# A two-layer block on one core: the first layer's last out projection placed among the third block's projections, and attention scores ordered behind the transposes of two units back

## What is computed

```python
# first layer
h = x @ w_in                                  # 1024 -> 3584
y = concat([sgu(...), conv(...), hgrn2(...)]) # each times silu(gate)
x = layernorm(ALPHA * x + y @ w_out)          # the out projection
# second layer
p = rmsnorm(x) @ w_in_2                       # 1024 -> 2560: pool input, q, k, v of both attentions
a = pool_mixer(...)
b = diff_attention(...)    # 4 heads: (softmax(q1 k1') - lam * softmax(q2 k2')) v, causal
c = stick_breaking(...)    # 4 heads, in pairs: sigmoid(z) times a reversed running product of 1 - sigmoid(z)
x = x + concat([a, b, c]) @ w_out_2
x = x + (silu(h2 @ w_gate) * (h2 @ w_up)) @ w_down ; out = rmsnorm(x)
```

## Time and profile before

| | |
|---|---|
| median of 3 runs | 3848.14 us (3844.67 to 3849.72) |
| profiled execution | 3846.98 us, its span 3844.6 us |
| mean granted TensorE clock | 0.988 of full speed |
| TensorE busy | 3722.9 us, 97% |
| VectorE, ScalarE, GpSimd busy | 1826.5, 1418.3, 476.1 us |

### The profile page before, as it was taken

The page is one execution under the profiler, slowest core; times in us unless marked ns, Lnnn a source line. Parts: engine busy times, 40 slices in busy tenths (PEclk is TensorE's granted clock), DMA queues, the critical chain, the costliest instruction groups (busy, mean ns, idle before and its releaser), DMA issues.

```text
span 3844.6 us, 58659 instructions
## 1 busy us (share of the span) xinstructions
PE 3722.9 (97%) x24136; PEld 3101.4 (81%) x24136; DVE 1826.5 (48%) x3358; ACT 1418.3 (37%) x2534; POOL 476.1 (12%) x244
## 2 busy tenths in 40 slices
PE   8989999999999989899999999999999999999999
PEld 7878878978897878787778887788888777887887
DVE  5757625551644353445665544555454454232223
ACT  4322422231232343465555545444455443021001
POOL 2102130000000000233433301000001000000000
PEclk9999999999999999899999999999999999999999
DMA  8746677557655858677677664455555333564554
GB/s 309 264 164 225 240 258 264 200 212 243 222 193 193 280 202 269 208 242 248 224 237 247 207 215 165 159 167 169 171 189 181 122 144 132 205 225 175 197 189 162
DMA packets 198874, 799.34 MB, mean 208 GB/s; under 512 B 20816, under 2 KB 70224, under 8 KB 130384
## 3 DMA queue, kind: packets, MB, share of 16 engines
q1 hardware_dynamic: 198608, 795.59, 59.4%
HBM read 594.18 MB, written 201.33 MB: 207 GB/s over the span
## 4 chain that ended last, share of the span: by engine, by line
PE 89%; DVE 4%; ACT 2%; DMA 2%; issue 1%; POOL 0%; SPq 0%; DVEq 0%; ACTq 0%
PE bank L1393 85%; PE bank L1397 4%; DVE P L2472 1%; DVE R L2133 0%; SPq L2676 0%; ACT L1927 0%; DMA Y2d<-PY 0%; ACT P L1928 0%; POOL slot L2636 0%; ACT P L1927 0%; DVE P L2474 0%; DMA zraw<-in_x_t_dram 0%; DMA R<-in_x_n_dram 0%; DMA slot<-Wd 0%; DVE small L2462 0%
## 5 line engine op out<-in xcount | busy, mean ns | idle before, releaser
L1393 PE MATMUL bank<-Z1a,slot 128*128 128x512 f32 x3048 | 785.0, 402 | 10.7 <-DVE slot L2071 9.5
L1393 PE MATMUL bank<-Z1b,slot 128*128 128x512 f32 x3048 | 786.8, 402 | 3.2 <-DVE Z1b L2180 3.2
L1393 PE MATMUL bank<-slot,Z0b 128*128 128x512 f32 (+1 forms) x3504 | 713.0, 353 | 14.8 <-DVE R L2133 12.0
L1393 PEld LDWEIGHTS bank<-Z1a,slot 128*128 128x128 f32 x3048 | 565.8, 190 | 141.3 <-DVE slot L2071 9.5
L1393 PEld LDWEIGHTS bank<-Z1b,slot 128*128 128x128 f32 x3048 | 567.4, 190 | 138.7 <-issue 8.7
L1393 PEld LDWEIGHTS bank<-slot,Z0b 128*128 128x128 f32 x3504 | 559.9, 188 | 110.5 <-DVE R L2133 16.6
L2636 POOL TENSOR_TENSOR slot<-raw,slot 128x1024 fp32r<-128x1024 f32 x117 | 295.9, 2536 | 714.3 <-ACT slot L1811 714.3
L2133 DVE SCALAR_TENSOR_TENSOR R<-bank,small,R 128x512 f32<-128x512 f32 x352 | 260.3, 748 | 207.5 <-PE bank L1393 207.0
L1393 PE MATMUL bank<-KS,DQ 128*128 128x512 f32 (+3 forms) x960 | 279.7, 390 | 23.5 <-ACT P L1928 11.8
L2440 DVE TENSOR_SCALAR_CACHE_REDUCE P<-bank 128x512 f32<-128x512 f32 (+3 forms) x320 | 187.7, 607 | 224.2 <-PE bank L1393 222.7
L2648 POOL TENSOR_TENSOR Z0b<-AF,Z0b 128x512 fp32r<-128x512 f32 x88 | 130.5, 1483 | 1282.1 <-ACT Z0b L2001 1282.1
(11 more groups left out here) (233 smaller groups left out, 4416.1 us busy)
## 6 DMA issues: line engine op xcount, KB each, us to landing
slot<-Wd SPq DMA_DIRECT2D x390, 1024.0 KB, 5.0
Wd<-slot SPq DMA_DIRECT2D x130, 1024.0 KB, 7.4
raw<-in_wts_dram SPq DMA_DIRECT2D x130, 512.0 KB, 4.2
DQ<-Qd SPq DMA_DIRECT2D x192, 128.0 KB, 3.7
DV<-Vd SPq DMA_DIRECT2D x60, 256.0 KB, 4.8
Kd<-QS SPq DMA_DIRECT2D x24, 512.0 KB, 5.2
Qd<-QS SPq DMA_DIRECT2D x24, 512.0 KB, 7.3
KS<-Kd SPq DMA_DIRECT2D x24, 512.0 KB, 7.0
```

The lines of the kernel that those rows point to most:

```text
L1393: return e.matmul(o, a, b, start=start, stop=stop, skip_group_check=True)
```

## The change

Seven things are edited. (1) The eight tiles of B for block 3 are used between tile 13 and 14 of C2 (`C_CUT`), and `phase_b(S - 1)` is called there from `phase_c`, no longer after it. (2) `front` may place the scores of unit u when the transposes of unit u - 2 are placed (`tr`, which free the buffer P), no longer when its output is copied out (`o`). (3) `SLACK_F` falls from 1000 to 300. (4) The planned VectorE time of a stick-breaking unit falls from 300 + 4.3 n to 300 + 3.5 n ns, n being its keys. (5) Q, K and V of blocks 1 and 2 are staged in `raw` (`staged`), those of 0 and 3 stay in `QS`, with waits to match: ScalarE waits once for the last first-use weights ahead of block 1, and the load of the first two E tiles waits for the stores of block 2 (`heads_stored`). (6) The load of residual rows (`r in`) is placed when the pooling of the block before is done. (7) The loops of `phase_c` are written as one. Instructions, their sizes and their numbers stay, and line numbers shift by up to 14 (L1393 is L1402 in the changed kernel, L1397 is L1406).

```diff
--- before.py
+++ after.py
@@ -40,6 +40,7 @@
 T_A, T_B, T_C, T_E, T_F = 0, 28, 36, 56, 64
 N_TILES = 64 + N_F
 NSLOT, NRAW = 4, 2
+C_CUT = 14
 
 
 class Signal:
@@ -172,9 +173,10 @@
     for s in range(S):
         for part in first_layer(s):
             order += TILES[part]
-        if s > 0:
+        if s == S - 1:
+            order += [*range(T_C, T_C + C_CUT), *range(T_B, T_B + N_B), *range(T_C + C_CUT, T_C + N_C)]
+        elif s > 0:
             order += range(T_C, T_C + N_C)
-    order += range(T_B, T_B + N_B)
     order += range(T_C, T_C + N_C)
     for s in range(S):
         order += range(T_E, N_TILES)
@@ -197,7 +199,7 @@
             for qt in range(NT)]
 
 
-SLACK_H, SLACK_C, SLACK_F, SLACK_B = 1500.0, 2000.0, 1000.0, 2500.0
+SLACK_H, SLACK_C, SLACK_F, SLACK_B = 1500.0, 2000.0, 300.0, 2500.0
 
 
 class Order:
@@ -533,7 +535,9 @@
 
 
     def phase_b(self, s):
-        self.dma(("r in", s), 2097152, self.P.end.get(("C gone", s - 1), 0.0))
+        if s:
+            yield ("pl y", s - 1, 1)
+        self.dma(("r in", s), 2097152, self.P.end.get(("pl y", s - 1, 1), 0.0))
         last = s == self.S - 1
         zr = [("zs", "Y", s, j) for j in (0, 1, 3, 2)]
         for cg in range(4):
@@ -587,17 +591,14 @@
                 yield ("pl halo", s - 1)
             yield from self.fm(("C", s, n), T_C + n, 1, zr, ("act", 610))
         P.add(self.pooling(s), slack=SLACK_C)
-        for n in range(2, 10):
-            yield from self.fm(("C", s, n), T_C + n, 1, zr, *kq)
+        for n in [*range(2, 10), 10, 12, *range(14, 18), 18]:
+            if (s, n) == (self.S - 2, C_CUT):
+                yield from self.phase_b(self.S - 1)
+            if n in (10, 12, 18):
+                yield from self.pair([("C", s, n, p) for p in range(2)], T_C + n, 1, zr, vv)
+            else:
+                yield from self.fm(("C", s, n), T_C + n, 1, zr, *kq)
             self.stored(s, n)
-        for n in (10, 12):
-            yield from self.pair([("C", s, n, p) for p in range(2)], T_C + n, 1, zr, vv)
-            self.stored(s, n)
-        for n in range(14, 18):
-            yield from self.fm(("C", s, n), T_C + n, 1, zr, *kq)
-            self.stored(s, n)
-        yield from self.pair([("C", s, 18, p) for p in range(2)], T_C + 18, 1, zr, vv)
-        self.stored(s, 18)
         P.put(("C done", s))
         yield ("pl y", s, 1)
         P.put(("C gone", s))
@@ -654,7 +655,7 @@
                     self.get(i, w)
                 self.get(i + 1, ("k", 0))
             if u > 1:
-                yield ("o", u - 2)
+                yield ("tr", u - 2, (NT * self.units[u - 2][0] + self.units[u - 2][3]) // 4)
             n = SUB * s + 128 * (qt + 1)
             ws = chunks(n)
             for r in ((0, 1) if e < 4 else (half,)):
@@ -682,7 +683,7 @@
                 P.put(("cb", u), ("dve", 900 + 1.1 * n), after=t)
             else:
                 yield t1
-                P.put(("cb", u), ("dve", 300 + 4.3 * n), after=t1)
+                P.put(("cb", u), ("dve", 300 + 3.5 * n), after=t1)
 
     def back(self):
         P = self.P
@@ -895,7 +896,6 @@
                 if s + 1 < S:
                     P.add(self.split_x(s + 1), True)
                 yield from self.phase_c(s - 1)
-        yield from self.phase_b(S - 1)
         P.add(self.split_y(0, "Y2"), True)
         yield from self.phase_c(S - 1)
         for s in range(S):
@@ -1045,12 +1045,16 @@
         def rows_of(x, s):
             return x[SUB * s:SUB * s + SUB, :].rearrange("(c p) n -> p c n", p=128)
 
-        def parts_of(i, n):
+        def staged(s, i):
+
+            return raw[i] if 0 < s < S - 1 else QS[i]
+
+        def parts_of(s, i, n):
 
             if n % 2:
-                x = QS[i][:, :].rearrange("p (c a t) -> p c a t", c=NT, a=2)
+                x = staged(s, i)[:, :].rearrange("p (c a t) -> p c a t", c=NT, a=2)
                 return x[:, :, 0, :], x[:, :, 1, :]
-            return QS[i][:, 0:SUB], QS[i][:, SUB:2 * SUB]
+            return staged(s, i)[:, 0:SUB], staged(s, i)[:, SUB:2 * SUB]
 
         def heads_of(b):
             return b[:, :].rearrange("p (c t) -> p c t", c=NT)
@@ -1290,11 +1294,16 @@
         def y2_out(s, e):
             return (d_y2p if e < 2 else d_py)("Y2 out", s, e)
 
-        def staging_stored(e, s):
+        def heads_stored(e, s):
 
             for i in range(2):
                 e.wait_ge(*d_qs[i](*[qkv_of[m] for m in sorted(qkv.values()) if qkv_of[m] in d_qs[i].at and qkv_of[m][1] == s][-1]))
                 e.wait_ge(*d_qv[i](*[qkv_of[m] for m in sorted(qkv.values()) if qkv_of[m] in d_qv[i].at and qkv_of[m][1] == s][-1]))
+
+        def staging_stored(e, s):
+
+            if s in (0, S - 1):
+                heads_stored(e, s)
             e.wait_ge(*y2_out(s, 1))
             e.wait_ge(*pe_pl("pl mm", s, 1))
 
@@ -1767,10 +1776,13 @@
                     act.wait_ge(*d_qs[i](*qkv_of[m - 2]))
                     if is_v(qkv_of[m - 2][2]):
                         act.wait_ge(*d_qv[i](*qkv_of[m - 2]))
+                if s == 1:
+                    for j in plan.news[:T_E][-NRAW:]:
+                        act.wait_ge(*weights_ready(j))
                 if is_v(n):
-                    to, x = QS[i][:, 0:SUB], b[:, :]
+                    to, x = staged(s, i)[:, 0:SUB], b[:, :]
                 else:
-                    to = parts_of(i, n)[0].bitcast(F32R)
+                    to = parts_of(s, i, n)[0].bitcast(F32R)
                     x = heads_of(b) if n % 2 else b[:, :]
                 e.activation(to, x, ACT.Copy).then_inc(*act_g.inc("ev", label))
 
@@ -2691,6 +2703,8 @@
 
             def weights(j):
                 if plan.first(j):
+                    if plan.tiles[j] in (T_E, T_E + 1):
+                        heads_stored(sp, S - 2)
                     if (k := plan.news.index(j)) >= NRAW:
                         sp.wait_ge(*weights_ready(plan.news[k - NRAW]))
                     transfer(raw[raw_of(j)][:, :], wts[plan.tiles[j]], d_raw[raw_of(j)], "wf", j)
...
```

8 lines of the change are left out of this document (4 added, 4 removed).

## The result

| | median of the runs, us | runs | against before |
|---|---|---|---|
| before | 3846.40 | 3844.12 to 3849.72 | |
| changed kernel | 3793.97 | 3792.94 to 3797.90 | ratio 0.9865, 95% interval 0.9848 to 0.9882 |

The changed kernel is 52.4 us faster. I had predicted 3807 us in a range of 3790 to 3835. The sign and the range held, and the size was 13 us short: it is the time of the rival "more than forecast" (3794).

What follows compares the result with a forecast made beforehand. TensorE, 97% busy, was taken to bound the kernel, with only its idle and half-clock time to gain. 18.0 + 1.95 + 26.0 - 5.7 = 40.2 us off 3846.98 gave 3806.7, predicted as 3807 us, range 3790 to 3835.

Steps and rivals of the forecast that it cites:

- more than forecast: Rival for the whole kernel: small waits don't grow and the third E tile gains its 7 us; 3794 us, chance 0.11.
- The end of B3: Post norm ahead of C3's transposes: 34.6 us of moved matmuls cover 17.4 us needed, so 18.0 us of loss goes.
- The residual rows: Load of R for B3: it waits for the pooling alone, so TensorE's wait goes; 1.95 us gained.
- The first E tile: Ten more units of attention lead let C3 projections cover block 0's store and read back; 26.0 us of loss goes.
- That the two gains can be added, each to its edit: Unsaid in the sum: 18.0 us at B3's end and 26.0 us at the first E tile were simply added.
- What the denser order costs: Attention with less main work beside it: 13 us more small waits, less 7.3 us at the third E tile; net 5.7 us.
- in proportion to the density: From 1610 to 3252 us: the 39.0 us of small idle times grow by 0.33 of themselves, 13 us.
- 7.3 us off for E2: With all attention placed ahead of this third E tile, its 9.2 us loss should fall to the fourth's 1.9 us.
- the sign that went with it: PE waits between the first E tile and the last attention matmul should sum to 40 to 60 us.
- Switching costs the same: On TensorE, the changed lists have as many kinds of alternation, so no change in switching cost.
- Slower, by scores ahead of their free banks: Rival in all units: scores listed before their banks are free stop main work too; 3855 us, chance 0.06.
- Half given back, by products slowed beside GpSimd: Rival in F0: slowed products and sigmoids hold the scores' banks, 20 us more; 3827 us, chance 0.17.

Runs made afterwards that it cites:

- e6_cut_18: The changed kernel with B3 put later, ahead of the last value pair (C_CUT 18 instead of 14); 3830.94 us, ratio 0.9953 to before.
- e1_move_only: The changed kernel with the three attention edits undone, leaving B3's new place and the raw staging of block 2; 3876.59 us, ratio 1.0069 to before.
- e4_slack_1000: The changed kernel with SLACK_F back at 1000 instead of 300; 3805.13 us, ratio 0.9885 to before.
- e3_output_key: The changed kernel with the old key: scores of unit u again behind the output copy of u - 2; 3833.64 us, ratio 0.9958 to before.
- e2_attention_only: The kernel before with the three attention edits (transpose key, SLACK_F 300, 3.5 n) and B3 in its old place; 3849.26 us, ratio 1.0.
- e15_key_only: The changed kernel with SLACK_F 1000 and 4.3 n put back, so the move and the new key stay; 3826.44 us, ratio 0.994 to before.
- e17_cost43_slackb1500: The changed kernel with 4.3 n put back and SLACK_B, the attention back end's slack, at 1500 instead of 2500; 3813.5 us, ratio 0.9903 to before.

## Why the prediction was right, and where it was off

- **The end of B3, 18.0 us.** Measured: 18.0 to 0. The cover was larger than I had counted (38.4 us from 1354.2 to 1392.6, not 34.6), and so was the need (26.0 us, not 17.4). Cover cut short brings the hole back (e6_cut_18). The step is right.
- **The residual rows, 1.95 us, bounds 0 and 2.** Wrong, though small. SP now issues the load at 1296.01, right behind a value store of block 2, and that is still late: VectorE waits 6.48 us for it (13.24 before) ahead of its first addition. The stretch up to the end of B3 loses 9.2 us where it lost 7.2.
- **The first E tile, 26.0 us.** Measured: 26.0 to 0. The reason given, more units placed ahead of block 0's end, agrees with the count of matmuls between the two ends. The price had a second part that the prediction didn't tell apart: 9.6 of the 26.0 us lay ahead of block 0's last value matmul.
- **That the two gains can be added, each to its edit.** This was unsaid in the sum, and it is wrong. Each hole goes with its own edit, but alone each opens as much elsewhere. That nothing opened elsewhere with both in place was taken for granted and not worked out, and there the sum was lucky. Had I been asked for the move alone, it would have said 3827 us; it is 3877.
- **What the denser order costs, 5.7 us.** This is the term that was mis-sized, and it is the larger part of the 13 us. I had taken the small waits in proportion to the density (39.0 x 1.33) and 7.3 us off for E2. Measured, with the clock loss: from the first E tile to the end 46.8 + 11.9 = 58.7 us before, 35.8 + 14.1 = 49.9 us after, so 8.8 us less and not 5.7 more. The step "in proportion to the density" failed, and so did the sign that went with it: idle time from the first E tile to the last attention matmul was to be 40 to 60 us and is 27.6. The density went up and the waits on VectorE's additions fell from 12.6 to 2.8 us, those on the sigmoids from 11.8 to 2.8. The other kernels don't bear out density either: the one whose attention ends latest (e1_move_only, 3250.9) loses most in this stretch, 55.6 us, and one that ends at 2926.1 (e4_slack_1000) least, 20.9. What does size these waits is only in part shown. Without the key the additions cost TensorE 10.5 us again (e3_output_key) but the sigmoids only 3.3, and two kernels with the key (e2_attention_only and e6_cut_18) lose 45.9 and 47.5 us there, to other waits. Against the 14.5 us of this term stand 2.0 us up to the end of B3, where I had forecast 1.95 us of gain, and 3.2 us in C3, which I had not forecast. That leaves 9 us of gain beyond the sum in the traces; the other 4 us of the 13 are that the profiled execution of the changed kernel is the slowest of its runs.
- **"Switching costs the same".** This says nothing of ScalarE, whose instructions did not stay in number. All 34 instructions that ScalarE is spared are table loads, rows ACT_TABLE_LOAD that stand ahead of its activations, 1.28 us each: 238 of them before and 204 now, 43.7 us of ScalarE's time. Those ahead of the stick-breaking sigmoids, before and in the changed kernel:

```profile
L1927 ACT ACT_TABLE_LOAD x42 | 53.9, 1283 | 17.9 <-DVE P L2465 8.9 <-DVE P L2474 8.4
```
```profile
L1939 ACT ACT_TABLE_LOAD x31 | 39.8, 1283 | 13.1 <-DVE P L2486 11.4 <-DVE P L2477 1.3
```

The saving comes mostly with the key: 237 in e1_move_only, 230 in e3_output_key, 210 in e15_key_only. It is a rival reason for the smaller waits on the sigmoids that no run separates from the order of the scores. It doesn't decide the time by itself: e2_attention_only has 212 and gains nothing.

- **Slower, by scores ahead of their free banks.** It didn't come: 2.8 us of waits on L1940 in the whole of 1610 to 2875. The change does have a slower side, but another one, which I had not listed: its first half alone.
- **Half given back, by products slowed beside GpSimd.** The products were slowed as the rival says, and it cost TensorE little. All 64 of them took 120.0 us where they took 109.6; the rival counted with 32 us more. Waits of ACT for the product, in before from 1610 to 3252, then in the changed kernel from 1588 to 2876:

```profile
ACT P L1927 <- DVE P L2474: 8.8, 2, 4.5
```
```profile
ACT P L1939 <- DVE P L2486: 57.3, 17, 5.7
```

ScalarE waited 57.3 us for products where it had waited 8.8, and TensorE 7.5 us (the list of its waits above). The products grew by 10.4 us in all, so most of ScalarE's longer wait is not in the products' own length. On the shared SBUF interfaces (the Trainium skill, GPSIMD Engine Reference, section Specifications) the trace agrees as far as it did in the earlier trace rows: the products are slowed. That TensorE lost only 7.5 us I put down to the other work in its row; no run tested it.

What stays open: why C3 loses 19.9 us in e1_move_only. Its waits there are read from the trace (5.9 us for VectorE's pooling tiles, 3.8 us without a named cause, 2.8 us for staged queries), but no run changed one of them alone. Which part of the smaller waits behind the first E tile is owed to the table loads is open as well. Open too is why changes of one number (e6_cut_18, e15_key_only, e17_cost43_slackb1500) cost 20 us and more outside the place they aim at.

## What to carry to other kernels

On an engine that works strictly in order, a latency is hidden by the work that stands between its two ends in the row: count that work at each hole, before and after a change, and see on which side of the first end the time is lost. Work put ahead of both ends left the hole as it was (39.6 and 38.6 us); the same amount between them took it from 26.0 to 16.4 us. Don't add up the gains of two order edits from a trace of the kernel without them: here +27 and 0 us made -52 together, so time the halves before judging either, and after such a change try the neighbouring numbers again (one of them put back gave 3787 us).

## What the hardware showed that I had not expected

Some small loads landed late where much else was in flight. DMA view of e1_move_only from 1560 to 1595 us:

```profile
DMA packets 3702, 9.48 MB, mean 271 GB/s; under 512 B 370, under 2 KB 1906, under 8 KB 3314
...
DV<-Vd SPq DMA_DIRECT2D x2, 256.0 KB, 14.9
```

Value rows of 256 KB took 14.9 us to land there. In the kernel before, the 60 loads of this kind from 1250 us on took 4.8 us at the median and 12.3 at most. TensorE waited 15.04 us for such rows in e1_move_only and 7.06 us in e2_attention_only. I read the long landing as the work of the larger transfers issued just ahead (rows of SP above); no run changed the order of issues alone.

Such a wait can go unnamed. In e6_cut_18 the 7.89 us ahead of the value matmul at 1636.59 are put down to "issue"; the two loads of its value rows were issued at 1626.6 and 1627.1 and took 9.9 and 10.1 us, which ends within 0.6 us of the matmul. I read it as that DMA; no run tested it.
